# Hybrid encoder layer on one core: neighbourhood attention with masked bias tables as one run per query and kind of columns, three bias transfers a head, and queries and keys as one transfer each

## The reference

```python
proj = h @ w_in                                  # u, q, k, v and two gates, h = rms_norm(x)
# neighbourhood_attention(q, k, v, rpb): 8 heads of 64; a query at (r, c) sees 8 rows x 16 columns, clamped to the grid
rs = jnp.clip(r - kr // 2, 0, rows - kr)
k_r = lax.dynamic_slice_in_dim(k, rs, kr, axis=1)[:, :, col_idx]
bias = rpb32[:, dr[None, :, None], dc[:, None, :]]
sc = jnp.einsum('bqhd,brqwhd->bhqrw', q_r, k_r).astype(jnp.float32) + bias[None]
p = jax.nn.softmax(sc.reshape(b, NA_HEADS, GRID_W, kr * NA_COL_WIN), axis=-1)
return jnp.einsum('bhqrw,brqwhd->bqhd', p, v_r)
# then x + W_out(sigmoid gates * (Fourier branch, attention branch)), and a convolutional feed-forward sublayer
```

## Time and profile before

| | us |
|---|---|
| median of 3 runs | 2887.94 (2884.75 to 2896.26) |
| profiled execution, its own time | 2883.12 |
| its span | 2881.3 |
| PE busy in the span | 2671.4 (93%) |
| DVE busy | 1599.6 (56%) |
| POOL busy | 764.9 (27%) |

### The profile page before, as it was taken

How to read it: one execution, slowest core, us unless ns; L and a number is a source line. 1 busy time by engine, 2 the same in 40 slices (tenths; PEclk the granted TensorE clock), 3 DMA queues, 4 the chain that set the end, 5 groups by cost and what they waited for, 6 DMA issues and landing times. The chain is left out here.

```text
span 2881.3 us, 33463 instructions
## 1 busy us (share of the span) xinstructions
PE 2671.4 (93%) x12528; PEld 2219.4 (77%) x12528; DVE 1599.6 (56%) x2490; ACT 853.2 (30%) x1519; POOL 764.9 (27%) x392
## 2 busy tenths in 40 slices
PE   6999999998959986999993999998999999999998
PEld 5888888887748875777783888886788888788876
DVE  5300000006459885544445899998655556685786
ACT  3311111112236652112113444443222223322242
POOL 2020011102132223433214666665000000332222
PEclk9999999999969998999996999999999999999999
DMA  4323134526555644655544777778566676996884
GB/s 144 99 84 81 56 124 141 166 69 229 186 153 163 178 138 142 196 181 163 165 133 158 286 278 271 273 275 281 200 220 223 223 249 218 308 331 215 273 290 166
DMA packets 241392, 556.93 MB, mean 193 GB/s; under 512 B 51540, under 2 KB 77008, under 8 KB 237520
## 3 DMA queue, kind: packets, MB, share of 16 engines
q1 hardware_dynamic: 219984, 533.83, 55.3%
q10 hardware_dynamic: 21248, 20.97, 2.1%
HBM read 371.15 MB, written 185.11 MB: 193 GB/s over the span
## 5 line engine op out<-in xcount | busy, mean ns | idle before, releaser
L2329 PE MATMUL ff_psum<-ff_w,ff_hid 128*128 128x512 f32 x1848 | 423.9, 392 | 12.3 <-DVE ff_y L2013 7.6
L2329 PEld LDWEIGHTS ff_psum<-ff_w,ff_hid 128*128 128x128 f32 x1848 | 349.2, 189 | 86.8 <-issue 11.0
L1867 POOL TENSOR_TENSOR ff_w<-ff_wraw,ff_w 128x512 fp32r<-128x512 f32 x154 | 279.5, 1817 | 230.9 <-ACT ff_w L2136 230.9
L422 PE MATMUL in_psum<-in_hA,in_w 128*128 128x512 f32 x1440 | 327.9, 389 | 0.0
L422 PEld LDWEIGHTS in_psum<-in_hA,in_w 128*128 128x128 f32 x1440 | 270.3, 188 | 56.1
L2282 PE MATMUL ff_psum<-ff_h,ff_w 128*128 128x512 f32 x1056 | 247.3, 394 | 39.9 <-DVE ff_h L1936 24.5
L2282 PEld LDWEIGHTS ff_psum<-ff_h,ff_w 128*128 128x128 f32 x1056 | 200.8, 190 | 83.0 <-POOL ff_w L1867 40.9
L2282 PE MATMUL ff_psum<-ff_h,ff_again 128*128 128x512 f32 x1056 | 246.5, 393 | 4.8 <-DVE ff_h L1936 4.2
L2282 PEld LDWEIGHTS ff_psum<-ff_h,ff_again 128*128 128x128 f32 x1056 | 199.9, 190 | 47.8 <-issue 4.6
L300 DVE CAST in_w<-in_raw 128x1024 fp32r<-128x1024 f32 x20 | 13.9, 693 | 394.8 <-PE in_psum L422 352.3
L1464 PE MATMUL mo_psum<-mo_act,mo_w 128*128 128x512 f32 x768 | 188.8, 403 | 35.9 <-POOL mo_act L1315 21.6
(11 more groups left out here) (191 smaller groups left out, 4191.8 us busy)
## 6 DMA issues: line engine op xcount, KB each, us to landing
split<-ff_w SPq DMA_DIRECT2D x154, 512.0 KB, 3.6
ff_again<-split SPq DMA_DIRECT2D x154, 512.0 KB, 4.1
ff_a_near<-hidden SPq DMA_DIRECT2D x67, 512.0 KB, 6.0
ff_wraw<-in_w_up_dram SPq DMA_DIRECT2D x44, 512.0 KB, 5.6
hidden<-ff_c SPq DMA_DIRECT2D x44, 512.0 KB, 3.2
at_bias<-shifted SPq DMA_DIRECT2D x72, 256.0 KB
ff_b_near<-in_w_down_dram SPq DMA_DIRECT2D x66, 256.0 KB, 6.6
ff_b_far<-in_w_down_dram SPq DMA_DIRECT2D x66, 256.0 KB, 6.1
```

What stands on the lines that cost most here:

```text
L422: last = nc.tensor.matmul(ps[:, bank], half(a, t)[:, k], hT(c, k, b * BLK, BLK), start=(k == 0 and (a, c) == SPLIT[0]), stop=(k == KD - 1 ...
L1867: nc.gpsimd.tensor_tensor(split_out(i, 1), parts(i), f32(split_out(i, 0)), ALU.subtract).then_inc(w_tail, 1)
L2329: last = nc.tensor.matmul(ps[:, tile_bank(i)], hid[:, q % SA, a, i * P:(i + 1) * P], w[:, (MADE + q) % RING, e], start=(k == 0 and (a, e) ...
```

## The change

1. **Tables made in the input phase.** The window mask goes into the tables: `padded` is filled with -1e30 from a constant and exists twice (rows and columns cut to the window, or full), `shifted` gets 46 rows instead of 31 and 63 copies instead of 48, four a block. A new DRAM tensor `tables` (3 kinds of columns x 8 x 8 heads x 16 x 40 x 32, 15.7 MB) is filled by 72 copies inside DRAM, over the last 28 blocks or so. It holds, for each query of a tile, one contiguous run of 5,120 bytes that serves all three kinds of rows.
2. **Three bias transfers a head** instead of nine: `load_bias(h, j)` reads 8 x 16 runs of 5 KB. `reduce` picks its 16 rows from the run, in one or two pieces; `masked_bias`, `window_kind` and their tensors are gone.
3. **Queries and keys one transfer each** (`load_raw`): the source pattern is [0, 2], [SEQ, 64], [1, SEQ], the destination 128 partitions. The queries wait only for `q_tail`, the keys for `k_tail`.
4. In head 0, ACT casts head 1's queries and keys at tiles 4 to 11 instead of 0 to 7.

```diff
 KIND = [0, 1, 1, 2]
 KINDS = 3
-REL_R, REL_C = 31, 64
+INNER_R, REL_R, REL_C = 31, 46, 64
...
+SHIFTS = [piece for j in range(KINDS) for c in range(QC)
+          for piece in (((j, c, 0, 0, KC),) if not FULL_C[j][0] <= c < FULL_C[j][1] else
+                        ((j, c, 1, FULL_C[j][2], COL_WIN), (j, c, 0, COL_WIN - FULL_C[j][2], COL_WIN)))]
+SPAN_R = KR + QR
+TAB_R = SPAN_R + 2 * ROW_WIN
+TABLES = [(j, r, dst, src, rows) for j in range(KINDS) for r in range(QR)
+          for dst, src, rows in ((ROW_WIN, r, SPAN_R),
+                                 (0 if r < 3 else ROW_WIN + SPAN_R, ROW_WIN + r, ROW_WIN),
+                                 (ROW_WIN + SPAN_R if r < 3 else 0, INNER_R + r, ROW_WIN))]
 NEG = -1.0e30
 
 
-def input_phase(nc, const_in, step, steps, low, raw, x, w_in, norm_g, b_gate, eye, rpb, u_out, qT_out, v_out, kT_out, gT_out, gate_w,
-                padded, shifted):
+def input_phase(nc, const_in, step, steps, low, raw, x, w_in, norm_g, b_gate, eye, rpb, mask, u_out, qT_out, v_out, kT_out, gT_out, gate_w,
+                padded, shifted, tables):
...
 
             def shift(n):
-                j, c = divmod(n, QC)
-                sp.dma_start(shifted[j, :, c], padded[:, :, BASE_C[j] - c:BASE_C[j] - c + KC]
+                j, c, full, k, run = SHIFTS[n]
+                at = BASE_C[j] - c + k
+                sp.dma_start(shifted[j, :, c, :, k:k + run], padded[full, :, :, at:at + run]).then_inc(padded_in, 16)
+
+            def table(n):
+                j, r, to, at, rows = TABLES[n]
+                src = shifted[j].rearrange("h q r c -> (h q) (r c)")[:, at * KC:(at + rows) * KC]
...
+            def bias_tables(m):
+
+                slots, cut = NG * GB - 2, len(SHIFTS) // 4 + 2
+                if m < cut:
+                    for i in range(4 * m, min(4 * m + 4, len(SHIFTS))):
+                        shift(i)
+                elif cut < m < slots:
+                    if m == cut + 1:
+                        sp.wait_ge(padded_in, 16 * (5 + len(SHIFTS)))
+                    n, of = m - cut - 1, slots - cut - 1
+                    for i in range(n * len(TABLES) // of, (n + 1) * len(TABLES) // of):
+                        table(i)
+
+            sp.dma_start(padded.rearrange("f h r c -> (f h r c)").rearrange("(p y) -> p y", p=P), mask).then_inc(padded_in, 16)
             for q in range(4):
                 if q >= 2:
...
+            sp.wait_ge(padded_in, 80)
...
+                    bias_tables(GB * t + b)
                     store(n, gT_out[t * P:(t + 1) * P, b * BLK:(b + 1) * BLK])
                     n += 1
...
 
...
-
-
-def attention_phase(nc, const_in, low, raw, qk_in, qT, kT, v, shifted, mask, eye, atT_out):
...
                       for i in range(3))
         vs = m.sb("vs", [P, 2, VG * TJ, HEAD_DIM])
-        bias = m.sb("bias", [P, 2, NB, KR * KC])
-        window = m.sb("window", [P, NB, KR * KC])
-        sides = m.sb("sides", [P, 256])
...
-            def load_bias(h, i):
-                for j in range(KINDS):
-
-
-                    rows = shifted[j, h]
-                    src = bass.AP(rows.tensor, rows.offset + (BASE_R[i] - (QR - 1)) * KC,
-                                  [[KC, QR], [REL_R * KC, QC], [1, KR * KC]])
-                    sp.dma_start(bias[:, h % 2, i * KINDS + j], src).then_inc(
-                        first_in if h == i == 0 else bias_in[h % 2], 16)
+            def load_bias(h, j):
+                src = bass.AP(tables.tensor, tables[j, 0, h].offset,
+                              [[HEADS * QC * TAB_R * KC, QR], [TAB_R * KC, QC], [1, TAB_R * KC]])
+                sp.dma_start(bias[:, h % 2, j], src).then_inc(bias_in[h % 2][j], 16)
 
...
 
+            def load_raw(h, dst, src, tail, landed):
+                sp.wait_ge(tail, whole(h - 1))
+                both = bass.AP(src.tensor, src[h * HEAD_DIM:(h + 1) * HEAD_DIM].offset, [[0, 2], [SEQ, HEAD_DIM], [1, SEQ]])
+                sp.dma_start(dst.rearrange("p r c -> p (r c)"), both).then_inc(landed, 16)
+
             def load(h):
                 if h:
-                    sp.wait_ge(q_tail, whole(h - 1))
-                    sp.wait_ge(k_tail, whole(h - 1))
-                    for half in range(2):
-                        for dst, src in ((qraw, qT), (kraw, kT)):
-                            sp.dma_start(dst[half * HEAD_DIM:(half + 1) * HEAD_DIM].rearrange("p r c -> p (r c)"),
-                                         src[h * HEAD_DIM:(h + 1) * HEAD_DIM, :]).then_inc(qk_in, 16)
+                    load_raw(h, qraw, qT, q_tail, qk_in)
+                    load_raw(h, kraw, kT, k_tail, k_in)
                 if h >= 2:
                     sp.wait_ge(s_red, TILES * (h - 1))
+                load_bias(h, 0)
                 if h == 0:
-                    load_bias(0, 0)
-                    load_values(0)
-                    load_bias(0, 1)
-                    load_bias(0, 2)
-                    return
-                for i in range(KINDS):
-                    load_bias(h, i)
+                    load_values(h)
+                load_bias(h, 1)
+                load_bias(h, 2)
                 if h >= 2:
                     sp.wait_ge(o_mm, TILES * (h - 1))
-                load_values(h)
+                if h:
+                    load_values(h)
 
             def store(pair):
...
                 pool.wait_ge(qk_heads, heads)
-                pool.wait_ge(window_done, 1 if heads == 3 else KINDS)
+                if heads > 3:
+                    pool.wait_ge(q_tail, 1)
                 G.tensor_tensor(qs[up, 0, rows], qraw[up, rows], f32(qs[up, 0, rows]), ALU.subtract).then_inc(q_tail, 1)
...
-                    pool.wait_ge(q_tail, 1)
-                    window_kind(0, 1)
-                    window_kind(0, 2)
             pool.wait_ge(q_tail, whole(0))
...
+            def bias_rows(tab, kind):
+
+                if kind == 1:
+                    rows = tab[:, (QR + QR // 2) * KC:(QR + QR // 2 + KR) * KC]
+                    return rows.rearrange("p (s e) -> p s e", s=2)
+                first = (0, None, ROW_WIN)[kind] * KC
+                both = tab[:, first:first + (SPAN_R + ROW_WIN) * KC]
+                return bass.AP(both.tensor, both.offset, [both.ap[0], [SPAN_R * KC, 2], [1, ROW_WIN * KC]])
+
             def reduce(n):
                 h, t, i, j = where(n)
                 dve.wait_ge(s_mm, n + 1)
-                kind = KIND[i] * KINDS + KIND[j]
-                dve.wait_ge(bias_ready, h * NB + kind + 1)
+                dve.wait_ge(bias_in[h % 2][KIND[j]], 16 * (h // 2 + 1))
                 if n >= 3:
                     dve.wait_ge(p_exp, n - 2)
-                V.tensor_tensor_reduce(out=neg[:, n % 3], in0=ps[:, SB[n % 3]],
-                                       in1=bias[:, h % 2, kind], scale=-1.0, scalar=3.0e38,
+                halves = [x.rearrange("p (s e) -> p s e", s=2) for x in (neg[:, n % 3], ps[:, SB[n % 3]])]
+                V.tensor_tensor_reduce(out=halves[0], in0=halves[1],
+                                       in1=bias_rows(bias[:, h % 2, KIND[j]], KIND[i]), scale=-1.0, scalar=3.0e38,
                                        op0=ALU.add, op1=ALU.min, accum_out=negmax[:, n:n + 1]).then_inc(s_red, 1)
 
...
-            def masked_bias(n):
-                h, t, i, j = where(n)
-                kind = KIND[i] * KINDS + KIND[j]
-                if i == 2 or j == 2:
-                    return
-                if h == 0:
-                    dve.wait_ge(window_done, kind + 1)
-                if h == 0 and kind < KINDS:
-                    dve.wait_ge(first_in, 16 * KINDS)
-                elif h % 2:
-                    dve.wait_ge(bias_in[1], 16 * NB * (h // 2 + 1))
-                else:
-                    dve.wait_ge(bias_in[0], 16 * (NB - KINDS) + 16 * NB * (h // 2))
-                b = bias[:, h % 2, kind]
-                V.tensor_tensor(b, b, window[:, kind], ALU.add).then_inc(bias_ready, 1)
-
             def first_k_tail(rows, heads):
                 dve.wait_ge(qk_heads, heads)
                 V.tensor_tensor(kl[:, 0, rows], kraw[:, rows], f32(kh[:, 0, rows]), ALU.subtract).then_inc(k_tail, 1)
 
...
             for n in range(-4, N):
                 if 0 <= n + 3 < N:
                     reduce(n + 3)
-                if 0 < n + 4 < N:
-                    masked_bias(n + 4)
                 if 0 <= n + 1 < N:
...
             def qk_head(h, part):
                 s = h % 2
                 r = slice(part % PARTS * ROWS // PARTS, (part % PARTS + 1) * ROWS // PARTS)
-                if part == (0 if h else PARTS):
-                    act.wait_ge(qk_in, 64 * (h + 1))
-                    if h >= 2:
-                        act.wait_ge(s_mm, TILES * (h - 1))
+                if h == 0:
+                    act.wait_ge(qk_in, 64)
+                elif part == 0:
+                    act.wait_ge(qk_in, 64 + 16 * h)
+                elif part == PARTS:
+                    act.wait_ge(k_in, 16 * h)
```

(6 more changed lines are left out.)

76 lines of the change are left out of this document (25 added, 51 removed).

## The result

The changed kernel takes **3069.6 us** (median of 4 runs, 3063.5 to 3070.8) against 2886.4 us before (2881.2 to 2896.3, 4 runs beside it): ratio 1.061, 95% interval 1.059 to 1.064. The prediction was 3050 us with a range of 3020 to 3092.

The account below looks back on a forecast made before the run. Two lowest DMA engines, slowed by queries and keys, would become attention's bound: 60.3 us a head against 29.0 of tiles. The last `reduce` moves 166.7 us, input phase 0: 2883.1 + 166.7 = 3049.8, forecast 3050 us, range 3020 to 3092.

Parts of the forecast that it names:

- What bounds the kernel now: Attention: PE fills quiet tiles; outermost source count sets a transfer's engines; the lowest are nearly full, 31.7 us for head 2.
- Queries and keys on two engines: Attention loads: outermost source count 2 gives two engines, at 26.1 GB/s each, 40.2 us a head for both.
- Bias at 25.6 GB/s an engine: Attention bias loads: three transfers over 8 engines, 245,760 B per engine, 9.6 us a head (11.5 before).
- The period: Attention, per head: 40.2 + 9.6 + 10.5 = 60.3 us on the two lowest engines, against 29.0 us of tiles.
- The path: Attention: keys of head 1 at 853.7, of head 7 at 1220.4; last `reduce` at 1265.0, 166.7 us later.
- Input phase: Table copies fit beside full PE: taken as 0, with +15 us as the bound above; ends at 653 as before.
- The signs named: Attention: DMA share near 0.13, ACT idle some 31 us a head, PE clock down to half, no stretched operation beside POOL.
- Removed `masked_bias`: Attention: 76.8 us of DVE gone, worth only POOL stops, 25 us, and less starting wait; lost if transfers come late.
- The first: Queries and keys: zero-step dimension folded away, transfers spread over 16 engines, PE the bound; 2830 us, chance 0.06.
- point of decision at 29 us: Attention: any engine count bringing the lowest engine's load per head under 29 us gives the gain.
- The second rival: Queries and keys: two engines at 13.4 GB/s each, 78.3 us for both, period 98.4; 3316 us, chance 0.03.
- the third: Attention loads: two engines, but other ones for each transfer; about today's pace, -5 us, 2878 us, chance 0.02.

Follow-up runs that it names:

- count-of-2 run: Changed kernel with queries and keys in two 64-row transfers each, rows dealt out under an outermost source count of 2, no zero step: 3083.9 us.
- halves: Changed kernel with queries and keys again as two transfers of 64 rows each: 2889.7 us, ratio 0.999.
- 128 different rows: Changed kernel, each queries or keys transfer reading 128 different rows (this head's and the next's) instead of 64 rows twice: 2852.7 us, ratio 0.986.
- another order at the start: Kernel with halves, values and bias over 16 engines; first head's second bias kind issued before its values, second head's casts from tile 1: 2830.4 us, ratio 0.978.
- the kernel before with one transfer: Kernel before the change, with only queries and keys made one transfer each with the zero step: 3101.6 us.
- one transfer with the rest on 16 engines: Changed kernel, queries and keys left as they are, values as 16 transfers of 32 rows and bias tables laid out by head: 3002.0 us, ratio 1.038.
- a count of 4: Changed kernel with queries and keys in two 64-row transfers each, rows dealt out under an outermost source count of 4: 2935.5 us.

## Why the prediction was right

The prediction was right: the direction, the mechanism, and the time within its range, 19.6 us above its figure.

- **What bounds the kernel now.** The count of engines was read from three plateaus and held for queries and keys at 2, with and without a step of zero, and at 4 without. The low engines did not run dry, as the prediction argued: no stretch of 2 us from 796 to 1240 has a share under 0.12. That the lowest engines were nearly full before was right too: relieving them of values alone gained 18.8 us with nothing of the change.
- **Queries and keys on two engines.** Right: 0.14 and 55 GB/s, inside the 50 to 54 foretold but for 1. The 26.1 GB/s for an engine was a little low: 53 GB/s at 0.13 in the count-of-2 run are 26.5, so 39.6 us rather than 40.2.
- **Bias at 25.6 GB/s an engine** is the term that was mis-sized. The row 905 to 922 shows 115 GB/s at 0.33 of 16, 21.8 for a busy engine, keys and bias together: an estimate of 11.3 us, not 9.6. The rate had been taken from one stretch in the earlier trace rows, and that one was fast for the kernel before as well. Cut its whole attention phase into stretches of 2 us: the 54 of them with a share of 0.47 to 0.56, where mostly bias moves, show 82 to 233 GB/s, 173 in the mean. This one is in its head 0:

```profile
826.00:834.00 8.00, 3.65 (x14) 2.95 (x14) 4.75 (x14) 0.00 (x0) 0.00 (x0) 0.50 0.51 104
```

- **The period**: 60.3 predicted, 62.6 measured, of it 0.8 us for the two stores that the prediction counted apart. The 1.5 us left are the two terms above (+1.7, -0.6) to within half a microsecond. That a rate too high did so little harm is in part luck of the case: bias is a sixth of this period. Where it is a third, with halves, the same rate led me to a wrong time.
- **The path.** Keys of head 1: 853.7 predicted, 863.25 measured, of which the later start of attention is 2.6 us (first issue at 793.39, not 790.77). Some 5 us more are bias again, as an estimate from 1.31 MB at 115 GB/s (11.4 us) where 205 (6.4 us) was assumed. This is the second and third kind for head 0:

```profile
806.00:814.00 8.00, 0.00 (x0) 0.00 (x0) 0.00 (x0) 0.00 (x0) 0.00 (x0) 0.50 0.52 115
```

  The 2 us left are open. Six periods and the stores: 366.7 predicted, 375.9 measured. Keys of head 7 to the last `reduce`: 44.6 and 42.6. Together 9.6 + 9.2 - 2.0 = 16.7 us, the distance from 1265.0 to 1281.7; 4.3 lie behind the attention phase, and the rest is the run against the median.
- **Input phase.** Taken as 0 and was: it ends at 653.8, before at 653.4 (SP's first issue of the next phase). But attention starts 2.6 us later. Of that 1.4 us are there when ACT begins with the position table in the Fourier phase (671.27, before 669.91); it was not tried whether the larger number of copies does this.
- **The signs named.** ACT's waits are 29.2 us a head, where some 31 were foretold; the granted clock is at half (0.50) in the row 806 to 814; `reduce` is not stretched (692 ns).
- **Removed `masked_bias`** gave nothing here, as said, since transfers came later than PE needed them. The runs bear out about the 25 us of it: with no transfer of queries or keys late, 42.3 - 18.8 = 23.5 us separate the kernels with and without it (the wait at the start and the form of the bias transfers differ as well).
- **The rivals.** The first (faster, 2830) supposed that the two-half form spreads over 16 engines. It did not. Its price, for bias on 8 engines and values on 4, is answered by the run nearest to it, that of 128 different rows: 2852.7, so 2830 was 22 us too low. Only with bias and values on 16 engines too, and another order at the start, did a kernel reach 2830.4. Its point of decision at 29 us held: no run whose low engines carried less than that waits longer than 0.79 us for queries or keys after head 0. The Trainium skill ("DMA: Bandwidth & Descriptors", Rules for kernel authors) advises to merge two transfers to partition halves; the trace agrees for 128 different rows (294 GB/s in one transfer) and contradicts it for 64 rows read twice through a step of zero. There its other rule decides, that the slowest count sets the engines: 55 GB/s. The second rival (13.4 GB/s an engine) was refuted by 55 GB/s on two engines, the third by the count-of-2 run.

**Where my own expectations failed.** For halves I summed 9.8 + 9.6 + 10.5 = 29.9 us and expected the tiles to set the pace; 35.9 were measured. With the bias at 11.3 the sum of loads meets the measured period for two engines (62.0 against 62.6) and nearly for four (20.1 + 11.3 + 10.5 = 41.9 against 43.1). It falls short by 4.3 for halves, 3.2 for the kernel before with one transfer (65.3 against 62.1, with its bias at 205 GB/s), and 5.4 for one transfer with the rest on 16 engines (53.0 against 40.2 + 4.8 + 2.6).

Most of this is the rate of the bias once more. In each run, take the mean of its own 2 us stretches with a share of 0.47 to 0.56: 140 GB/s with halves, 157 with a count of 4, 170 in the kernel before with one transfer. As estimates, the bias then takes 14.0, 12.5 and 13.9 us, and the sums are 34.3 (measured 35.9), 43.1 (43.1) and 63.9 (65.3). So the sum of loads meets these three within 1.6 us if the rate is a mean over many stretches, in which mostly bias moves; one plateau is a poor source for it. The 5.4 us with the rest on 16 engines stay unexplained.

Why bias transfers of one form move anything from 82 to 233 GB/s is open. Distance of planes as tried (5 KB more changed nothing) and length of rows (409 GB/s with 5 KB over 16 engines; slow stretches with 2 KB too) do not explain it. Low engines that hold pieces of several transfers at once would look like this, and no run took it apart.

## What to carry to other kernels

Write the source of a DMA so that its slowest dimension has many entries: 2, 4 and 8 gave as many engines, 32, 64 and 128 came with all 16, and nothing between 8 and 32 was tried. Read the share of busy DMA engines in a stretch in which that transfer is alone: it tells the engines at once, as 2/16, 4/16 or 8/16. Add up bytes for the busiest engine, not for the queue, and compare with the compute of the period. Take the rate from the mean of many stretches, not from one. Merging two transfers into one by a leading dimension of 2 took 16 engines down to 2 here, and 187 to 215 GB/s down to 55; a gain elsewhere in the same change shows only once the fullest engine is below the compute.
